# Expert mixer: the weighted sum of gathered value rows moved from one full TensorE array to four 64x64 blocks of it

## The reference, cut to what matters

```
x = rmsnorm_input + mixers ...                       # residual stream, (tokens, 1024)
h = rmsnorm(x, norm_ffn_w)
idx, g = route(h)                                    # 128 expert numbers and gates per token
u = u_tab[ib]                                        # gathered rows
act = gelu(einsum('thkd,td->thk', u, xb))            # one dot product per token and slot
v = v_tab[ib]
out = einsum('thk,thkd->td', (gb * act).astype(v.dtype), v)
x = x + out
y = rmsnorm(x, final_norm_w)
```

## Time and profile before

| | us |
|---|---|
| median of 2 runs | 4730.47 |
| the two runs | 4730.15, 4730.79 |
| span of the profiled execution | 4728.8 |

### The profile page before, as it was taken

The page is one execution under the profiler, slowest core; times in us unless marked ns, Lnnn a source line. Parts: engine busy times, 40 slices in busy tenths (PEclk is TensorE's granted clock), DMA queues, the critical chain, the costliest instruction groups (busy, mean ns, idle before and its releaser), DMA issues.

```text
span 4728.8 us, 44920 instructions
## 1 busy us (share of the span) xinstructions
PE 3724.3 (79%) x12914; PEld 1960.8 (41%) x12914; DVE 2737.7 (58%) x5963; ACT 691.1 (15%) x1844; POOL 1485.7 (31%) x1547
## 2 busy tenths in 40 slices
PE   8999590745469994887977978978878879779777
PEld 5767460723334443432532523534424325325221
DVE  1000529158831114687686785785886876867865
ACT  1110120112223220101101111111111011011110
POOL 3000310401100000444444443454444444444442
PEclk9999755867679997999999999999999999999999
DMA  4111300121131112999999999999999999999998
GB/s 161 61 40 36 75 2 2 47 95 41 34 152 67 54 44 105 411 412 395 413 418 390 415 419 393 412 421 394 416 419 394 416 413 392 415 389 414 420 401 360
DMA packets 253462, 1271.34 MB, mean 269 GB/s; under 512 B 62096, under 2 KB 92432, under 8 KB 113168
## 3 DMA queue, kind: packets, MB, share of 16 engines
q0 software_dynamic: 156672, 1140.92, 58.6%
q1 hardware_dynamic: 96576, 127.93, 8.1%
HBM read 1226.22 MB, written 40.09 MB: 268 GB/s over the span
## 4 chain that ended last, share of the span: by engine, by line
DMA 23%; PE 21%; DVE 8%; issue 7%; POOL 2%; ACT 0%; POOLq 0%; DVEq 0%; SPq 0%; ACTq 0%
DMA pe_ring<-in_uv,pe_index_now 20%; PE pe_acc L1832 15%; PE pe_ps_q L1803 5%; DVE pe_ring L1757 2%; DMA pe_ring<-in_uv,pe_index 2%; POOL pe_ring L1576 2%; DVE pe_work_a L1640 2%; DVE pe_diag L1745 1%; DVE pe_picked L1722 1%; PE pe_ps_s L1813 1%; PE pe_acc L1819 0%; DMA pe_w_q<-in_w_q 0%; DVE pe_top L1699 0%; ACT pe_square L1621 0%; DVE pe_dot L1757 0%
## 5 line engine op out<-in xcount | busy, mean ns | idle before, releaser
L1832 PE MATMUL pe_acc<-pe_ring,pe_diag 128*128 128x512 f32 (+1 forms) x4352 | 2069.4, 618 | 451.7 <-DVE pe_diag L1745 451.1
L1576 POOL DMA_INDIRECT pe_ring<-in_uv,pe_index_now x1024 | 1211.9, 1184 | 1304.8 <-PE pe_acc L1832 1120.5
L1757 DVE CUSTOM_DVE_ANT_0 pe_ring<-pe_ring,pe_h_now 128x1024 f32<-128x1024 f32 x1024 | 1252.7, 1224 | 553.4 <-DMA pe_ring<-in_uv,pe_index_now 550.7
L1832 PEld LDWEIGHTS pe_acc<-pe_ring,pe_diag 128*128 128x128 f32 (+1 forms) x4352 | 786.6, 192 | 1636.7 <-DVE pe_diag L1745 908.2
L1617 ACT ACTIVATE pe_act_v<-pe_dot 128x1 f32<-128x1 f32 x1088 | 220.6, 203 | 2395.1 <-DVE pe_dot L1757 2390.2
L1745 DVE TENSOR_SCALAR pe_diag<-pe_ident,pe_act_v,pe_gate_now 128x128 f32<-128x128 f32 x1024 | 355.3, 347 | 56.3 <-DVE pe_top L1686 7.4
L1803 PEld LDWEIGHTS pe_ps_q<-pe_h_t,pe_w_q 128*128 128x128 f32 x2304 | 280.7, 194 | 63.8 <-issue 61.2
L1803 PE MATMUL pe_ps_q<-pe_h_t,pe_w_q 128*128 128x128 f32 x2304 | 281.5, 277 | 2.2 <-DMA pe_w_q<-in_w_q 2.2
L372 PE MATMUL pj_bank<-pj_w_in,pj_normed_t 128*128 128x512 f32 (+1 forms) x720 | 267.7, 529 | 5.6 <-DMA pj_w_in<-in_w_in 5.6
L1392 PE MATMUL mo_ps_out<-mo_w_out,mo_both_t 128*128 128x512 f32 x576 | 251.2, 594 | 14.7 <-DVE mo_both_t L1342 11.9
L378 PE MATMUL pj_bank<-pj_normed_t,pj_w_in 128*128 128x128 f32 x1728 | 195.2, 276 | 0.0
(11 more groups left out here) (302 smaller groups left out, 3083.0 us busy)
## 6 DMA issues: line engine op xcount, KB each, us to landing
pe_ring<-in_uv,pe_index_now POOLq DMA_INDIRECT x1024
pe_w_q<-in_w_q SPq DMA_DIRECT2D x4, 2048.0 KB, 19.9
m2s_window<-scratch_xbc SPq DMA_DIRECT2D x8, 786.0 KB, 5.1
pj_w_in<-in_w_in SPq DMA_DIRECT2D x1, 6144.0 KB, 38.6
scratch_xbc<-pj_chan_out SPq DMA_DIRECT2D x8, 768.0 KB, 5.1
pj_x<-in_x_all SPq DMA_DIRECT2D x9, 512.0 KB, 4.7
scratch_u<-pj_token_out SPq DMA_DIRECT2D x9, 512.0 KB, 2.6
scratch_z<-pj_token_out SPq DMA_DIRECT2D x9, 512.0 KB, 3.7
```

Source lines behind the costliest of these rows:

```text
L1576: nc.gpsimd.indirect_dma_start(out=ring[:, s, :], out_offset=None, in_=D["uv"], in_offset=bass.IndirectOffsetOnAxis(ap=row, axis=0)).then_ ...
L1757: last = V.tensor_tensor_reduce(out=ring[:, s, 0:D_MODEL], in0=ring[:, s, 0:D_MODEL], in1=tokens[:], scale=1.0, scalar=0.0, op0=ALU.mult, ...
L1832: last = T.matmul(acc[0:width, b, :], diag[:, s, 0:width], ring[:, s, D_MODEL + b * 512:D_MODEL + b * 512 + 512], start=False, stop=False)
```

## The change

Slots are taken in pairs (`GROUP` 2, so the ring has 4 groups of 2 slots, and a step of routing comes with every group). `diag` is 128x64: 64 columns of a folded identity, so rows 0 to 63 hold the diagonal for tokens 0 to 63, and rows 64 to 127 that for tokens 64 to 127. PE multiplies 64 rows by 64 columns at a time. For each half of the 1024 values there are four such matmuls: slot a low to low and high to high, slot b low to high and high to low. `acc` takes four banks instead of two (which leaves one bank each to `ps_q` and `ps_s`). At the end of a tile ACT copies the two crossed partial sums to the other half of the partitions, and DVE adds `x_now` and the partial sums into `out`; PE's `add_x` is gone. The norm then reads `out` from SBUF.

```diff
-    RING, GROUP = 8, 1
+    RING, GROUP = 8, 2
-    ROUTE_LINKS, END_LINKS = UNITS * 4 + 28, 2
+    ROUTE_LINKS, END_LINKS = UNITS * 4 + 28, 4
-        diag = sb("diag", [P, RING, P])
+        diag = sb("diag", [P, RING, SAMPLE])
-        acc = ctx.enter_context(nc.psum_tensor("pe_acc", [P, 2, 512], F32))
+        acc = ctx.enter_context(nc.psum_tensor("pe_acc", [P, 2, 2, 512], F32))
-        ps_q = ctx.enter_context(nc.psum_tensor("pe_ps_q", [P, 2, UNIT, P], F32))
-        ps_s = ctx.enter_context(nc.psum_tensor("pe_ps_s", [P, 2, UNIT, P], F32))
+        ps_q = ctx.enter_context(nc.psum_tensor("pe_ps_q", [P, 1, UNIT, P], F32))
+        ps_s = ctx.enter_context(nc.psum_tensor("pe_ps_s", [P, 1, UNIT, P], F32))
+        low, high = slice(0, SAMPLE), slice(SAMPLE, P)
+        part_sum = lambda rows, turn: acc[rows, turn].rearrange("p b c -> p (b c)")
...
 ACT, end of a tile:
-                act.wait_ge(tile_done, k + 1)
-                A(square[:], acc[:].rearrange("p b c -> p (b c)"), ACT.Square, accum_out=end_stat[:, 0:1]).then_inc(end_summed, 1)
+                act.wait_ge(group_done, RING_GROUPS + k * GROUPS + groups)
+                A(square[low], part_sum(high, 0), ACT.Copy)
+                A(square[high], part_sum(low, 1), ACT.Copy).then_inc(crossed, 1)
...
+                act.wait_ge(sum_ready, k + 1)
+                A(square[:], out[:], ACT.Square, accum_out=end_stat[:, 0:1]).then_inc(end_summed, 1)
...
 DVE, in weigh and at the end of a tile:
-                        last = V.tensor_scalar(diag[:, s, 0:width], eye[:], act_v[:, s:s + 1], gates[:, col:col + 1], ALU.mult, ALU.mult)
+                        last = V.tensor_scalar(diag[:, s, :], fold_ident[:], act_v[:, s:s + 1], gates[:, col:col + 1], ALU.mult, ALU.mult)
...
+                dve.wait_ge(group_done, RING_GROUPS + k * GROUPS + groups)
+                dve.wait_ge(y_out, 16 * k + 16)
+                dve.wait_ge(x_now_ready, k + 1)
+                tt(out[low], x_now[low], part_sum(low, 0), ALU.add)
+                end.link(tt(out[high], x_now[high], part_sum(high, 1), ALU.add))
+                dve.wait_ge(crossed, k + 1)
+                if more:
+                    end.link(tt(out[:], out[:], square[:], ALU.add))
...
+                dve.sem_inc(acc_free, 1)
+                dve.sem_inc(sum_ready, 1)
...
 PE:
-                        if n >= 2 and j % UNIT == 0:
-                            pe.wait_ge(q_ready, UNITS * r + n - 1)
+                        if n >= 1 and j % UNIT == 0:
+                            pe.wait_ge(q_ready, UNITS * r + n)
...
-                pe.wait_ge(x_now_ready, k + 1)
-                pe.wait_ge(y_ready, k + 1)
-                add_x(0)
+                pe.wait_ge(acc_free, k + 1)
...
-                    for s in slots:
-                        for b in range(2):
-                            last = T.matmul(acc[0:width, b, :], diag[:, s, 0:width], ring[:, s, D_MODEL + b * 512:D_MODEL + b * 512 + 512],
-                                            start=False, stop=False)
+                    for b in range(2):
+                        for turn, s in enumerate(slots):
+                            for i, rows in enumerate((low, high)):
+                                to = (low, high)[i ^ turn]
+                                last = T.matmul(acc[to, i, b, :], diag[rows, s, :], ring[rows, s, D_MODEL + b * 512:D_MODEL + b * 512 + 512],
+                                                start=g == 0, stop=g == groups - 1)
...
-                add_x(1).then_inc(tile_done, 1)
```

More of the change, by code:

```diff
@@ L1603, in route @@
                         act.wait_ge(q_made, UNITS * r + n + 1)
-                        A(q_t[:, n % 2], ps_q[:, n % 2], ACT.Copy).then_inc(q_ready, 1)
+                        A(q_t[:, n % 2], ps_q[:, 0], ACT.Copy).then_inc(q_ready, 1)
                     if g == SCORE_COPY + UNIT * n:
                         act.wait_ge(s_made, UNITS * r + n + 1)
-                        A(score[:, UNIT * n:UNIT * n + UNIT, :], ps_s[:, n % 2], ACT.Copy).then_inc(s_ready, 1)
+                        A(score[:, UNIT * n:UNIT * n + UNIT, :], ps_s[:, 0], ACT.Copy).then_inc(s_ready, 1)
                 if g == EXP:
@@ L1619, in tile @@
                         route(k + 1, g // EVERY)
-                act.wait_ge(tile_done, k + 1)
-                A(square[:], acc[:].rearrange("p b c -> p (b c)"), ACT.Square, accum_out=end_stat[:, 0:1]).then_inc(end_summed, 1)
+                act.wait_ge(group_done, RING_GROUPS + k * GROUPS + groups)
+                A(square[low], part_sum(high, 0), ACT.Copy)
+                A(square[high], part_sum(low, 1), ACT.Copy).then_inc(crossed, 1)
+                if not more:
+                    act.wait_ge(folded_in, 1)
+                    A(square[low], part_sum(high, 1), ACT.Copy).then_inc(crossed, 1)
+                act.wait_ge(sum_ready, k + 1)
+                A(square[:], out[:], ACT.Square, accum_out=end_stat[:, 0:1]).then_inc(end_summed, 1)
                 act.wait_ge(end_summed, k + 1)
@@ L1738, in tile @@
                     chain.start(ROUTE_LINKS * (k + 1))
[L1739 removed]
+                tokens, gates = (h_now, gate_now) if more else (h, flat_gate)
                 def weigh(g):
@@ L1809, in route @@
                         pe.wait_ge(q_ready, UNITS * r + n + 1)
-                        if n >= 2:
-                            pe.wait_ge(s_ready, UNITS * r + n - 1)
+                        if n >= 1:
+                            pe.wait_ge(s_ready, UNITS * r + n)
                         for j in range(UNIT):
-                            last = T.matmul(ps_s[:, n % 2, j, :], q_t[:, n % 2, j, :], keys_t[:, UNIT * n + j, :], start=True, stop=True)
+                            last = T.matmul(ps_s[:, 0, j, :], q_t[:, n % 2, j, :], keys_t[:, UNIT * n + j, :], start=True, stop=True)
                         last.then_inc(s_made, 1)
-            def add_x(half):
-                for b in range(2):
-                    last = T.matmul(acc[:, b, :], half_ident[:, half, :], x_now[:, b * 512:b * 512 + 512], start=half == 0, stop=half == 1)
-                return last
             def tile(k, groups, more):
-                width = P if more else SAMPLE
-                pe.wait_ge(x_now_ready, k + 1)
-                pe.wait_ge(y_ready, k + 1)
-                add_x(0)
+                pe.wait_ge(acc_free, k + 1)
+                settle(pe, settled)
                 for g in range(groups):
```

26 lines of the change are left out of this document (16 added, 10 removed).

## The result

| | us |
|---|---|
| changed kernel, median of 2 runs | 5320.53 (5317.76, 5323.3) |
| kernel before | 4730.47 |
| ratio, with its 95% interval | 1.1251 [1.1218, 1.1284] |
| profiled span, changed kernel | 5315.1 |

The forecast was 4980 with a range of 4800 to 5180. The direction was right, the size was two fifths of what came: +590 us where +250 was forecast.

A forecast was written before the change was run, and what follows sets the result against it. DMA's gather pace, 2.49 us a slot, was taken as the bound, with slot holding the question. Low-clock losses of 24.6 + 9.5 - 1.2 in each of 8 tiles plus 15 gave 5007 us; 85% of the way there gave 4980, range 4800 to 5180.

The forecast's parts named there:

- 4T = landing + T + dots + R + P: Ring loop from a pair's issue to the issue four pairs on, T per pair; also 0.81 us from PE's end to issue.
- R: Routing time between a pair's dots and diagonals; some 1.5 us with waits per routing step, the heaviest over 2.29.
- P: PE's time for a pair's 16 records; four blocks at once, 1.98 us at the upper clock level, 3.37 at the lower.
- 5.57 us. Both slots of a pair: 2.49 later, 8.06: Landing in the ring loop: issue to one slot seen by DVE 5.57 us, to both slots of a pair 8.06.
- the 85% step: Final total taken 85% of the way to the low-clock sum of 5007 us, from the upper-level 4839, giving 4980.
- The clock: PE's clock expected at its lower level, 1.2 GHz, outside the query steps; upper level back in them, as PE works through.
- The passage: Change between tiles, where DMA runs dry: longer by 6.4 us at the upper clock level, 9.5 at the lower.
- Not slower: Rival, 9%: the loop stays under the ring and only passages between tiles cost, if P + R is below 2.9 us; 4779 us.
- Two at a time: Rival, 15%: PE runs two blocks at a time, P = 3.70 us at the upper clock level; 5096 us.
- three times the rate: Rival, 6%: four blocks at three times the rate of one, at the low clock level, P = 4.5 us; 5177 us.
- one after another: Rival, 6%: PE's blocks run singly, P = 7.1 us bounds every pair; 6200 us.
- the first: First named sign: dots per pair spaced 5.1 us instead of 4.98 in a quiet stretch, about 5.6 in the searches.

The follow-up runs named there:

- weighing in turn: Changed kernel with each pair weighed behind its own dots and routing step, not behind the next pair's: 4773.45 us, 1.0095.
- own waits: Changed kernel with one landing semaphore per slot instead of per pair, so the first slot's dot need not wait for the second: 5147.48 us, 1.0885.
- a ring of 16: Changed kernel with 16 slots, weights and keys cut to make room: 4704.32 us, 0.9952; kernel before with the same: 4697.74 us, 0.9934.
- the ring of 4: Kernel before with 4 single slots instead of 8, each still weighed after the next one's dot: 6249.34 us, 1.3236.
- the filler: Changed kernel with two more full-array matmuls on zero weights behind pairs outside the query steps, to keep TensorE busy: 5247.26 us, 1.1114.
- the ring of 4 weighed in turn: Kernel before with 4 single slots instead of 8, each weighed in its own turn: 5583.13 us, 1.1773.
- the pairs on the full array: Kernel before with GROUP 2 and nothing else, so slots in pairs on the full 128x128 array: 5559.32 us, 1.1758.
- 8 records of two blocks: From the changed kernel with GROUP 1: single slots, two 64x64 blocks at a time, no crossed sums: 4792.18 us, 1.0138.

## Why the prediction was right and wrong

The loop can be read step by step. The means below are of my own adding up, over the slots of seven tiles, from the starts of instructions and packets in the trace of the changed kernel; "pred." is at the lower level for quiet stretches and searches, at the upper for queries. The prediction's 4.6 and 5.18 for queries were meant for the seven query steps that have searches; for the other nine it took 3.1 and no loss.

```
us                                quiet          searches       queries
                                  pred.  after   pred.  after   pred.  after
issue to first packet of slot a          2.85           2.70           3.38
first packet of a to that of b           2.92           2.96           2.83
first packet of b to a's dot             4.77           4.57           4.50
landing of a pair                 8.06   10.54   8.06   10.23   8.06   10.71
dots, routing, diagonals          3.1    2.84    4.6    4.55    4.6    3.57
TensorE and on to the issue       4.25   4.37    4.25   4.25    2.86   3.42
sum / 3                           5.14   5.92    5.64   6.34    5.18   5.90
spacing of pairs, measured               5.87           6.34           5.82
```

- **That the hold of a slot decides, and 4T = landing + T + dots + R + P: right.** What shows it is the experiments: weighing in turn, own waits, and a ring of 16 each take out what the loop says must go. That the sum closes is weaker evidence, as its terms were measured along the loop itself. Its sum with the measured terms gives the measured spacing within 0.1 in all three columns, and in the single slots of the ring of 4 (6.16 + 1.56 + 3.47 = 11.19, / 3 = 3.73, measured 3.70).
- **The landing of a pair, "5.57 us. Both slots of a pair: 2.49 later, 8.06": this is the step that failed.** It is 10.2 to 10.7. The 5.57 came from an empty queue (and was the shortest of seven) and the 2.49 from a full one, and neither holds in a thin one. Even behind the empty queue of the passage a pair takes 9.2, as its second slot comes 3.0 behind the first. In the loop the first packet of a pair then comes 2.7 to 3.4 after the issue instead of 1.7. The packets of its second slot take 3.7 us from first to last (3.7 for single slots with the ring of 4, 2.9 before), and the common wait ends only with the last of them. 2.2 to 2.7 us more in the landing are 0.7 to 0.9 a pair, after the division by 3.
- **What that is in the total.** A tile grew by 69.3 us (332.9 to 402.1) where the sum had 32.9: 36.4 too little, 291 in eight tiles, of the 335 us that the forecast lacked. It lies within the tile: the sum had 5.36 a pair on average (4.98 + 24.6/64), measured are 6.1 over the 59 pairs outside the passage, some 43 us, less 6, as the kernel before stood at 5.08 and not at 4.98. Another 27 are the 85% step, which should have been the whole way, and 17 the sample tile with its end and 2 us ahead of the stage (32 measured, 15 predicted).
- **P, "I take four at once": right.** 1.95 and 3.69 us at the two levels against 1.98 and 3.37. The Trainium skill (TensorEngine Tiling, Tiling Modes) says four tiles work in parallel, and this trace agrees; the 3.07 times of its page TensorE: Matmul & The Clock Gate (Part 3) does not fit here, as two slots in four blocks take the time of one on the full array. That page gives the figure for four tiles of 32 rows, which this kernel does not have, so the prediction carried it over to another packing.
- **The clock: right in the main outside the query steps, wrong in them.** PEclk was 0.71 and 0.73 there, not near 5 tenths. A pair takes TensorE 3.2 to 3.3 us in the mean (3.37 predicted), as about one in seven runs at the upper level throughout. From step 24 on, the granted clock averaged 0.59 while TensorE worked on a pair and 0.79 between pairs: much of the upper level falls into TensorE's waits. In the query steps it was 0.87 and not 1.00, as TensorE was busy for 73.5 of 95 us and did not work through. The rule of the Trainium skill (TensorE: Matmul & The Clock Gate, HAM oscillation) that bursts between DMA waits fall back to half clock agrees, with TensorE's waits of 5.48 us and the 3.69 us behind them; the filler shows that it was worth some 73 us, not the loss.
- **One support for the clock was misread.** The "5.61 of 20 us" at 0.50 is line L607 alone. All of TensorE was busy for 19.48 us of that window, so it says nothing of what pauses do:

```profile
600.00:620.00 20.00, 19.48 (x87) 12.27 (x83) 4.07 (x10) 4.39 (x20) 4.26 (x15) 0.50 0.02 2
```

- **Dots, routing and diagonals: right within 0.3.** Quiet 2.84 (3.1), searches 4.55 (4.6). The 3.57 of the query column is a mean of 2.95 in the nine steps without searches (3.1 predicted) and 4.37 in the seven with them (4.6). But those nine steps lost time as well, 5.7 a pair where 4.98 was summed: there too the landing was the long term.
- **The passage, "+9.5": the sum right, partly by luck.** +9.7. Its terms, as means of seven: from the landing to TensorE's end and on to the square 5.5 longer (6.9 predicted), from the first dot to the first refill 3.2 longer (2.6), and the first pair's landing 9.2 us where 5.8 + 2.49 would be 8.3, another 0.9. The last is the failed term again, made up for by the first.
- **Rivals.** "Not slower" had its point at P + R = 2.9: P alone was above it at the lower level, and the landing came on top. Two at a time, three times the rate and one after another all fall by the 1.95 us. Of the signs that the forecast named, the first did not come: quiet spacing was 5.87 and not 5.1, in the searches 6.34 and not 5.6.

## What to carry to other kernels

When a ring of buffers is filled by a queue, write the loop from the issue of a buffer to its next issue, and divide it by the number of groups. A step that is done "one group late" adds a whole spacing to the loop, so it takes one group out of the divisor: here three instead of four, and each other term costs a third per pair. Making the group larger without making the ring larger doubles that step in time. Before trusting such a sum, take the landing from a stretch in the same state as the one forecast: put together from an empty and a full queue it was too short by a quarter here. If the loop must be shortened, do first what adds next to no work: weigh in turn (547 us here), wait for each slot by itself (173 us).

## What the runs showed of the hardware

- With few gathers in the queue the DMA engines move less for each unit of their busy share: 413 GB/s with a ring of 16 (share 1.00), 378 in the changed kernel (336 at 0.89), 365 in the ring of 4 weighed in turn (310 at 0.85) and 357 in the other (268 at 0.75). It does not follow the share alone: the pairs on the full array have 388 at 0.80 (310 GB/s).
- That is not every packet being slower. Over tiles 2 to 8 a packet of 8 KB took 317 ns in the mean before and 367 with the ring of 4, weighed late, but the median is 312 and 309. What grows is a tail: with the ring of 4, 11% of the packets take over 0.5 us, against 0.8% before. Seven in ten of these 11% are among the first 16 of the 128 packets of their slot, whose mean is 0.63 us (before 0.32). So there it is mostly the start of a gather that is slow. In the changed kernel 6.6% take over 0.5 us, one in three of them among the first 16. Why they are slow stays open.
- A 64x64 block of fp32 runs beside three others at no loss: 16 records of 512 columns in 1.95 us, as long as 8 records of two blocks (1.93) and 4 records of the full array (1.98).
- More TensorE work can make a kernel faster: 1628 filler records, 861 us of busy time, a clock of 0.90 instead of 0.74, and 73 us less.
